# A decoder step on one core: the ninth tile's normalised rows made on POOL and ScalarE, its root moved between slot operations, and more identity products

## The reference, cut to what matters

```python
def channel_mixer(x, norm_g, w_group, w_expert, w_gate, w_up, w_down):
    n = rms_norm(x, norm_g).reshape(B * T, D)
    return x + hier_moe(n, w_group, w_expert, w_gate, w_up, w_down).reshape(B, T, D)
# hier_moe: logits = n @ [w_group | w_expert]; the best of 4 groups, the best 2 of its 8 experts;
# every expert e takes the rows that chose it:  (silu(xb @ w_gate[e]) * (xb @ w_up[e])) @ w_down[e]
```

## Time and profile before

| | us |
|---|---|
| median of three runs | 1125.38 (1125.37 to 1125.92) |
| the profiled execution's own time | 1126.27 |
| its span in the profile | 1124.5 |
| PE busy, whole span | 1093.6 (97%) |
| DVE, ACT, POOL busy | 444.9, 330.1, 171.1 |

### The profile page before, as it was taken

How to read it: one execution, slowest core, us unless ns; L and a number is a source line. 1 busy time by engine, 2 the same in 40 slices (tenths; PEclk the granted TensorE clock), 3 DMA queues, 4 the chain that set the end, 5 groups by cost and what they waited for, 6 DMA issues and landing times.

```text
span 1124.5 us, 26890 instructions
## 1 busy us (share of the span) xinstructions
PE 1093.6 (97%) x11636; PEld 799.3 (71%) x11636; DVE 444.9 (40%) x833; ACT 330.1 (29%) x648; POOL 171.1 (15%) x149
## 2 busy tenths in 40 slices
PE   8999999999999999999999999999999999999995
PEld 7999999966665559999766666666666666666663
DVE  6326654378875543345722212212212222122121
ACT  6323332266775552223211111111111111111111
POOL 0001200599100000000001111111111111111110
PEclk9999999999999999999899999999999999999998
DMA  7356684000126468464699999999999999999991
GB/s 240 112 154 210 219 274 124 1 13 2 38 76 188 120 218 292 151 254 177 259 345 403 384 384 386 393 373 386 392 376 389 388 389 385 388 387 386 385 348 33
DMA packets 85695, 293.05 MB, mean 261 GB/s; under 512 B 13375, under 2 KB 44799, under 8 KB 59957
## 3 DMA queue, kind: packets, MB, share of 16 engines
q1 hardware_dynamic: 78405, 273.69, 64.9%
q0 software_dynamic: 7168, 17.58, 6.7%
HBM read 272.98 MB, written 42.87 MB: 281 GB/s over the span
## 4 chain that ended last, share of the span: by engine, by line
PE 90%; DVE 3%; DMA 3%; ACT 2%; issue 1%; POOL 0%; SPq 0%; ACTq 0%; POOLq 0%; DVEq 0%
PE bank L2084 14%; PE bank L2500 11%; PE bank L2504 10%; PE bank L2508 9%; PE bank L2315 8%; PE bank L2534 5%; PE bank L2538 5%; PE bank L2542 4%; PE bank L2127 4%; PE bank L2292 3%; PE bank L2256 3%; PE bank L2165 2%; PE bank L2479 2%; DMA wo_raw<-in_w_out 2%; PE bank L2520 1%
## 5 line engine op out<-in xcount | busy, mean ns | idle before, releaser
L2500 PE MATMUL bank<-w_ring,xeT 128*32 128x256 f32 x1536 | 342.6, 380 | 0.0
L2504 PE MATMUL bank<-w_ring,xeT 128*32 128x512 f32 x1536 | 265.7, 594 | 0.7 <-ACT xeT L1493 0.7
L2500 PEld LDWEIGHTS bank<-w_ring,xeT 128*32 128x32 f32 x1536 | 166.2, 110 | 54.2
L2534 PE MATMUL bank<-w_ring,hT 128*32 128x256 f32 x768 | 171.7, 380 | 0.0
L2508 PE MATMUL bank<-w_ring,xeT 128*32 128x256 f32 x1536 | 155.8, 379 | 0.0
L1966 DVE SCALAR_TENSOR_TENSOR hid<-sgl,gtab,bank 96x256 f32<-96x256 f32 x32 | 21.9, 685 | 338.0 <-ACT sgl L1499 338.0
L2538 PE MATMUL bank<-w_ring,hT 128*32 128x512 f32 x768 | 133.2, 595 | 1.6 <-ACT hT L1505 1.6
L2084 PE MATMUL bank<-w_hi,xh 128*128 128x256 f32 (+1 forms) x432 | 124.6, 288 | 2.5 <-DVE xl L1566 2.4
L2084 PE MATMUL bank<-w_hi,xl 128*128 128x256 f32 (+1 forms) x432 | 121.7, 282 | 0.0
L2084 PE MATMUL bank<-w_lo,xh 128*128 128x256 f32 (+1 forms) x432 | 121.6, 282 | 0.0
L1702 DVE TENSOR_TENSOR_SCAN keep<-keep,unseen 128x1024 f32<-128x1024 f32 (+7 forms) x64 | 94.5, 1509 | 39.2 <-ACT keep L1284 39.1
(11 more groups left out here) (277 smaller groups left out, 1643.1 us busy)
## 6 DMA issues: line engine op xcount, KB each, us to landing
w_ring<-in_w_gate SPq DMA_DIRECT2D x64, 1024.0 KB
w_ring<-in_w_up SPq DMA_DIRECT2D x64, 1024.0 KB
w_ring<-in_w_down SPq DMA_DIRECT2D x64, 1024.0 KB
k_scr<-in_cache_k SPq DMA_DIRECT2D x32, 256.0 KB, 3.4
v_scr<-in_cache_v SPq DMA_DIRECT2D x32, 256.0 KB, 3.5
pgk<-k_scr SPq DMA_DIRECT2D x32, 256.0 KB, 4.0
w_raw<-in_w_in SPq DMA_DIRECT2D x7, 1024.0 KB, 7.1
pgv<-v_scr SPq DMA_DIRECT2D x4, 1024.0 KB, 7.0
```

What stands on the lines that cost most here:

```text
L2500: return pe.matmul(up_right_ps(i, g), xeT[i][:, k, rows_of(g)], w[1][:, k, FA:F], start=first and g != 1, stop=ends, skip_group_check=True)
L2504: pe.matmul(gate_ps(i)[rows_of(g), :], xeT[i][:, k, rows_of(g)], w[0][:, k, :], start=first, stop=ends, skip_group_check=True)
L2534: return pe.matmul(y_right_ps(g), hT[:, ft, rows_of(g)], w[:, ft, DA:D], start=first and g != 1, stop=ends, skip_group_check=True)
```

## The change

For the ninth tile DVE no longer writes `xg`. POOL writes `xmid * gffn` into it as soon as `xmid` is done, and ACT, after the root and DVE's inverse, scales it in place by `rs`. DVE's two small operations of the norm move into `place_slots(2)`: the mean between the reduction of the ranks and the first table operand, the inverse behind the last one. PE has twelve identity products ahead of `ranks(3)` in place of eight, and six ahead of `tables(3)` in place of five. A semaphore is dropped and its count put onto another.

```diff
@@ POOL, behind the last constant
+            r = ROWS[LAST]
+            pool.wait_ge(s_xm, tile_done(LAST))
+            pool.wait_ge(s_nst[LAST % 2], 16 * (LAST // 2))
+            rows = [a.rearrange("r (p k) -> r p k", p=P) for a in (xmid[0:r, LAST, :], gffn[0:r, :])]
+            pool.tensor_tensor(xg[LAST % 2][0:r, :].rearrange("r (k p) -> r p k", p=P), rows[0], rows[1], ALU.mult).then_inc(s_ng, 1)
@@ ACT
             root_mid(LAST)
+            r, i = ROWS[LAST], LAST % 2
+            act.wait_ge(s_ng, 1)
+            act.wait_ge(s_rms2, NT + 1)
+            act.activation(xg[i][0:r, :], xg[i][0:r, :], ACT.Copy, scale=rs[0:r, i:i + 1]).then_inc(s_n2, 1)
             exps(3)
@@ DVE
+            def last_root():
+                r, c = ROWS[LAST], slice(LAST % 2, LAST % 2 + 1)
+                dve.wait_ge(s_ssq2, NT)
+                dve.tensor_scalar(ss[0:r, c], ss[0:r, c], 1.0 / D, EPS, ALU.mult, ALU.add).then_inc(s_ms2, 1)
+                return r, c
+
+            def last_inverse(r, c):
+                dve.wait_ge(s_rms2, NT)
+                dve.reciprocal(rs[0:r, c], rs[0:r, c]).then_inc(s_rms2, 1)
@@ place_slots(q, with_root=False)
                 chain.link(dve.reduce_sum(rk[:, :, ts], prod[:, :, 0:n, :], axis=AXX))
+                if with_root:
+                    of_last = last_root()
                 ...
                 dve.tensor_tensor(named[:, :, :, NE:2 * NE], ek[:, :, 0:n, :], each(gt[:, :, ts], NE), ALU.mult).then_inc(s_ohr, 1)
+                if with_root:
+                    last_inverse(*of_last)
+                    dve.wait_ge(s_rms2, NT + 1)
@@ norm_scale(t)
                 if t == LAST:
-                    place_slots(2)
+                    place_slots(2, with_root=True)
+                    return
@@ PE
-            keep_warm(8)
+            keep_warm(12)
             ranks(3)
-            keep_warm(5)
+            keep_warm(6)
             tables(3)
@@ the router's constants: s_tbl dropped, counted on s_wg
-                      allow_small_or_imprecise_dtypes=True).then_inc(s_tbl, 1)
+                      allow_small_or_imprecise_dtypes=True).then_inc(s_wg, 1)
-                    dve.wait_ge(s_tbl, 1)
+                    dve.wait_ge(s_wg, 2)
-                    pe.wait_ge(s_tbl, 1)
+                    pe.wait_ge(s_wg, 2)
```

More of the change, by code:

```diff
@@ L542, in hybrid_step @@
     s_wr = sem("router_weights_loaded")
-    s_wg = sem("router_gain_applied")
-    s_tbl = sem("router_tables_ready")
+    s_wg = sem("router_prepared")
+    s_ng = sem("last_rows_times_gain")
     s_zr = sem("last_logits_cleared")
@@ L1835, in mark, with place_slots @@
                 last.then_inc(s_eb, 1)
-            def place_slots(q):
+            def last_root():
[6 more added lines that the diff above has]
+                dve.reciprocal(rs[0:r, c], rs[0:r, c]).then_inc(s_rms2, 1)
+            def place_slots(q, with_root=False):
                 lo, hi = BATCHES[q]
```

## The result

The changed kernel takes 1127.89 us (median of 20 runs, 1126.29 to 1130.50), the kernel before 1125.56 beside it (20 runs, 1124.15 to 1127.42). The ratio of the two is 1.0022, with a 95% interval of [1.0016, 1.0028]: slower by some 2.4 us. The time lies inside the stated range, 1.9 above the stated 1126.0, and just beyond 1127.6, from where the prediction counts "slower" (chance 0.16).

The account below looks back on a forecast made before the run. PE's fixed run of experts, some 550 us, was taken as the bound, its start set by the chain ahead. DVE -2.17, stall +2.51, PE's effects and 0.6 at the experts gave +0.6 on 1125.4: 1126.0, range 1123.6 to 1128.4.

Parts of the forecast that it names:

- What bounds the kernel: Experts' part: one expert is 17.10 us of busy PE, so a shift of its start passes to the end one for one.
- Part 1: DVE ahead of the ninth tile's logits: relieved of 2.17 us, logits scaled at 548.47 if taken alone.
- Part 2: POOL's product, taken as 2.8 us, stalls DVE's line 1844 by 2.51 us; logits 0.34 later than before.
- Rival A: DVE and POOL don't meet behind the ninth sum: full 2.17 us gained, -1.9 up to -2.4, 1123.3 us; chance 0.10.
- Rival C: POOL's strided write is slow, its product 4.3 us instead of 2.8: DVE +1.5 more, 1127.5 us; chance 0.16.
- Part 3: ACT's scaling pass (1.06 us) and the ninth tile's stores, about 1 us later, stay hidden: cost nothing.
- Part 4: PE idles 1.5 us before tables(2); clock rises during the twelve products; last operand 1.1 later, table about unchanged, -0.1.
- rival B: Clock stays at half through the twelve products: tables(3) 3.4 us later (3.0 with POOL at 2.4), 1128.6 us; chance 0.14.
- The first expert's start: PE idles 2 us before the gathered rows, first expert's products may start at half clock: 0 to 1.5, taken 0.6.
- The sum: DVE -2.17, stall +2.51; last operand +1.1, tables(3) gives back 1.2; experts' start +0.6: about +0.6 us, 1126.0.

## Why the prediction was right or wrong

**What bounds the kernel: right.** An expert stays at 17.10, and what moves the start moves the end.

**Part 1, DVE relieved of 2.17 us: right.** With POOL's product all but gone, the logits come at 3.39 us; before at 5.59. That is 2.20.

**Part 2, POOL holds DVE: right in mechanism and place, too large in size.** Line 1864 lasts 2.17 to 2.19 in the four traces with the whole product. The size of POOL's product was 2.36 and not 2.8: the strided output costs POOL nothing that can be seen, 2.36 to 2.38 against 2.38 for a plain one. So the logits are 0.2 earlier than before, not 0.34 later. By the Trainium skill ("SBUF — State Buffer", "SBUF: two separate sides") the later engine blocks for the whole instruction; the measured ends, 0.03 us apart, agree, and the cuts agree with "instruction": the hold shrinks with its length. Rival A, no collision, is refuted by the trace (its price was about right: with the stall taken away the ratio is 0.9984, 1.8 us faster, against the 1.9 to 2.4 that it gave). Rival C is refuted by the 2.36; the rule on strided access that it names from the same page of the Trainium skill ("Door 1: The DMA port swizzle", box on cachelines) shows on DVE and not on POOL.

**Part 3, ACT and the stores: right.** Cost nothing, ACT's pass 1.15 and not 1.06.

**Part 4, the clock under the twelve products: the step that was mis-sized.** The gap came (1.25 to 1.27, forecast 1.5), and the clock fell. I let it return "some way through the twelve" with ranks(3) 11.05 us after the ninth sum and the table unchanged. It returned only near their end: 11.83, 11.99 and 11.90 us in the three traces with twelve products and the whole stall, the table +0.85 in the first. That is nearly rival B's mechanism, which put the ranks at 12.65 and was to decide if the twelve ended after 557, that is 11.95 us after the ninth sum, with more than four fifths of them at half clock. The three traces lie around that moment, and on B's side by the share: the twelve took 5.2 to 5.4 us where 2.8 is full clock and 5.5 half, so some nine tenths of them ran at half. But its consequence did not come: the clock was up again for the six products, 1.58 us against rival B's 2.8, and for tables(3), 0.55. So tables(3) began 1.1 later than before, a third of rival B's 3.4.

**The first expert's start, for which I took 0.6 of 0 to 1.5: too small.** It was 1.7 in both traces of the changed kernel that have ten products there. In nine traces PE waited 1.8 to 2.2 us for the gathered rows, and in seven of them the first half took 6.9 to 7.0 instead of 5.3; before, half-clock products happened to fill that wait.

**The sum.** Forecast +0.6: at the table -0.1, at the expert +0.6, and the rest rounding. In the traces +0.85 at the table, the expert 0.3 earlier than before and its half 1.7 longer: +1.4. The medians say +2.3, against the kernel before whose own executions vary by 3 us. Of the 0.9 between them 0.7 is that the traced execution of before lay 0.7 above its own median; what was slower in it is not shown. There was luck in the distance to the stated time: with POOL's measured 2.36 in place of 2.8 the same sum would have come out 0.4 lower, so one term too large hid part of those too small. (Rival B's 1128.6 is 1125.4 and some 3.2, which lies between the 3.4 and 3.0 that its text gives.) What the experiments add is that the two parts are not a sum: products alone -0.2, root alone +0.2, POOL and ACT with the old products +0.2, each uncertain by 1 us, and everything together +2.4 to +2.9.

## What to carry to other kernels

An idle POOL is not free help for DVE. In these runs a POOL product on SBUF held a DVE operation of only two columns with constants, and others with two SBUF inputs, until its instruction ended, while a reciprocal beside it kept its 0.17 us and a sum that reads PSUM its 0.42. Look for DVE operations of the held kinds right behind the place, and cut POOL's work into short instructions. A small stall on the feeding engine can cost twice, as it did here, if it opens a gap on TensorE and the filler work behind that gap then runs at half clock in front of something urgent. The same filler cost nothing without the gap. Filler where TensorE waits for a transfer did no harm, and probably helped.

## What the runs showed of the hardware that was not expected

POOL's product of 1,024 columns with its output 128 numbers apart lasted 2.36 to 2.38 us, the same as a plain one. Eight POOL instructions of 128 columns next to DVE's operations took 3.99 us in all where one took 2.36, and DVE's operations were 0.10 to 0.22 longer than by themselves. Behind a 1.25 us gap the clock was granted at 0.50 in every window of one us from 552 to 558 of the changed kernel, though PE was fully busy from 553 on; with eight and five products it was at 0.50 in every such window from 550 to 566, with PE fully busy from 551. With 18 instead of ten products in the later wait it stayed at full in both traces that had them, but two of the nine traces with a wait of 1.8 us and more there had the fast first half too.
